# An output layer whose first groups are staged differently and an attention layer that keeps v in the matmul array

## What is computed

```python
# first block, layer 1: convolution mixer
c = layer_norm(depthwise_conv(glu(h @ w_in)))           # norm over the 1024 channels
y = (silu(c) * silu(z)) @ w_out + b_out                 # the "output layer" of this text
h = layer_norm(ALPHA * h + y)
# first block, layer 2: gated linear attention, then h = layer_norm(...)
# second block: banded attention (8 heads of 64, 2 kv heads) beside a pooling branch
def banded_attention(q, k, v, rel_bias, sink):          # blocks of 128 queries, 384 keys each
    s = where(|rel| <= 128, q @ k.T * scale + bias, -1e30)
    m = maximum(max(s), sink)
    p = exp(s - m); p = p / (sum(p) + exp(sink - m))
    return p @ v
a = banded_attention(...) * silu(gate)
x = x + rmsnorm(concat(a, pool) @ w_out)
```

## Time and profile before

| | |
|---|---|
| median of 3 runs | 2679.57 us (2676.35 to 2681.12) |
| the profiled execution, its own time | 2668.11 us |
| its span, first to last instruction | 2666.4 us |
| mean granted clock of PE | 0.964 of full |
| PE, DVE, ACT, POOL busy | 2470.5, 1361.8, 1123.5, 737.0 us |
| `conv_out`, about | 559 to 856 us of the span |
| `attn_mix`, steps of attention | 1889.9 to 2267.7 us of the span |

### The profile page before, as it was taken

One profiled execution on the slowest core, in us unless ns is written; L12 is line 12 of the kernel. 1 busy time (PEld: TensorE's weight loads), 2 busy tenths in 40 slices (PEclk: granted clock), 3 DMA queues, 4 the chain that ended last, 5 costly groups with the idle time before them and its releaser, 6 DMA issues. The chain is left out here.

```text
span 2666.4 us, 34476 instructions
## 1 busy us (share of the span) xinstructions
PE 2470.5 (93%) x13014; PEld 1330.6 (50%) x13014; DVE 1361.8 (51%) x2287; ACT 1123.5 (42%) x2180; POOL 737.0 (28%) x516
## 2 busy tenths in 40 slices
PE   7999999768998999999999998997999998898898
PEld 3555555433444455555555554443666665343343
DVE  3998888964444233434334334774355555234322
ACT  5665554455553333434334334333345544222311
POOL 0788777545776110110111010441000000000000
PEclk9999999978999999999999999998999998899899
DMA  5011110041323100100000003232200000100322
GB/s 185 25 41 54 40 40 28 16 149 59 103 95 142 52 1 5 48 1 32 13 5 9 1 1 127 95 127 59 55 17 9 8 0 1 36 16 1 128 101 94
DMA packets 48813, 134.49 MB, mean 50 GB/s; under 512 B 5071, under 2 KB 19023, under 8 KB 47640
## 3 DMA queue, kind: packets, MB, share of 16 engines
q1 hardware_dynamic: 48664, 132.47, 14.7%
HBM read 96.65 MB, written 35.80 MB: 50 GB/s over the span
## 5 line engine op out<-in xcount | busy, mean ns | idle before, releaser
L388 DVE SCALAR_TENSOR_TENSOR cm_tap_sum<-cm_glu,cm_prm,cm_tap_sum 128x2048 f32<-128x2048 f32 x168 | 395.6, 2354 | 49.2 <-ACT cm_tap_sum L246 44.5
L315 POOL TENSOR_TENSOR mixed<-mixed,cm_tap_products 128x2048 f32<-128x2048 f32 x71 | 325.7, 4588 | 88.7 <-ACT cm_tap_products L267 72.6
L90 PE MATMUL cm_proj<-H_hi,cm_w_ga_hi 128*128 128x416 f16 (+1 forms) x640 | 217.8, 340 | 21.9 <-DVE H_lo L362 18.6
L91 PE MATMUL cm_proj<-H_lo,cm_w_ga_hi 128*128 128x416 f16 (+1 forms) x640 | 217.9, 340 | 0.0
L92 PE MATMUL cm_proj<-H_hi,cm_w_ga_lo 128*128 128x416 f16 (+1 forms) x640 | 217.6, 340 | 0.0
L90 PE MATMUL gm_vr<-gm_wvr_hi,H_hi 128*128 128x512 f16 (+1 forms) x544 | 208.9, 384 | 0.0
L91 PE MATMUL gm_vr<-gm_wvr_lo,H_hi 128*128 128x512 f16 (+1 forms) x544 | 208.8, 384 | 0.0
L92 PE MATMUL gm_vr<-gm_wvr_hi,H_lo 128*128 128x512 f16 (+1 forms) x544 | 208.8, 384 | 0.0
L1389 POOL TENSOR_TENSOR gm_q_inter<-gm_q_rel,gm_block_decays 128x512 f32<-128x512 f32 x16 | 16.7, 1047 | 497.1 <-ACT gm_block_decays L1466 497.1
L1732 DVE SCALAR_TENSOR_TENSOR gm_v_r<-gm_vr,gm_v_r 128x256 f32<-128x256 f32 (+1 forms) x68 | 28.8, 424 | 243.1 <-ACT gm_v_r L1483 243.1
L260 ACT ACTIVATE cm_tap_products<-cm_glu,cm_prm 128x2048 f32<-128x2048 f32 x64 | 125.8, 1993 | 36.5 <-POOL mixed L315 36.5
(11 more groups left out here) (358 smaller groups left out, 5821.0 us busy)
## 6 DMA issues: line engine op xcount, KB each, us to landing
cm_w_stage<-conv_w SPq DMA_DIRECT2D x24, 512.0 KB, 4.0
co_rows<-x_rows SPq DMA_DIRECT2D x16, 512.0 KB, 4.4
h_rows<-co_rows SPq DMA_DIRECT2D x16, 512.0 KB, 2.9
mixed<-gla_w SPq DMA_DIRECT2D x8, 1024.0 KB, 7.0
go_rows<-h_rows SPq DMA_DIRECT2D x16, 512.0 KB, 4.0
h_rows<-go_rows SPq DMA_DIRECT2D x16, 512.0 KB, 2.8
fo_rows<-h_rows SPq DMA_DIRECT2D x16, 512.0 KB, 3.6
out<-fo_rows SPq DMA_DIRECT2D x16, 512.0 KB, 2.6
```

The source lines that it names most:

```text
L90: nc.tensor.matmul(out, w_hi, x_hi, start=first, stop=False)
L91: nc.tensor.matmul(out, w_hi, x_lo, start=False, stop=False)
L315: nc.gpsimd.tensor_tensor(c_tile(j), c_tile(j), prod[:, r % 2, :], ALU.add).then_inc(s_add, 1)
L388: nc.vector.scalar_tensor_tensor(out=acc[:, :], in0=window(j, k), scalar=col(j, k), in1=acc[:, :], op0=ALU.mult, op1=ALU.add).then_inc(s_t ...
```

## The change

In `conv_out`: the weights arrive in two transfers, columns 0 to 511 under a semaphore of their own. DVE makes both the high and the low half of the weights, the first four channel tiles before the first group's variance and the rest behind its norm. `stats` makes all eight sums of c first and then the eight sums of squares; group 1 has PSUM banks of its own for them (those of output row 1), so its sums need not wait for the norm of group 0, and output row 1 waits instead until group 1 is normed (`c_n`). The first two squares of groups 2, 3 and 4 stand ahead of the row's own work in ACT's list.

In `attn_mix`: v is the stationary operand (64 columns per head, the two heads side by side in the array) and the transposed probabilities stream past (128 columns), so the output comes out transposed and `oT` and `p_o` are gone. The division by the sum is made on the probabilities, by POOL, before they are transposed. The sink is one more column of the scores (a zero column in PSUM, the sink in the bias), so its exponential and its sum come with the others. Scores are negated, so one minimum gives the bias of the exponential. The low half is stored by POOL. The steps overlap deeper: in step U PE makes scores(U), outputs(U-3), half a projection, probsT(U-2), half a projection. All quarters project q of the next group in their first two steps and the gate in their last two; in the last group the gate is spread over four steps. All 64 steps are written out in place of the register loop.

```diff
+                sp.dma_start(w_out_room(H_hi)[:, :, 0:512], w_out_rows(next_w)[:, :, 0:512]).then_inc(ahead.half, 16)
+                ahead.load(sp, w_out_room(H_hi)[:, :, 512:D], w_out_rows(next_w)[:, :, 512:D])
...
-                def split_w(h):
-                    for k in range(KT):
-                        c = slice(h * 512, h * 512 + 512)
-                        nc.scalar.activation(w_hi[:, k, c], w_in[:, k, c], ACT.Copy, scale=WS).then_inc(s_wh, 1)
-
                 def next_squares(k):
-                    for i in ((2 * k - 8, 2 * k - 7) if k >= 4 else ()):
-                        square(1, i)
+                    if k + 2 < KT:
+                        square(1, k + 2)
                 for k in range(KT):
                     square(0, k)
-                act.wait_ge(ahead.sem, loaded)
-                split_w(0)
+                square(1, 0)
+                square(1, 1)
                 mean_square(0)
...
+                    if s in STATS:
+                        square(STATS[s], 0)
+                        square(STATS[s], 1)
...
-                    if T:
+                    if T >= 2:
                         pe.wait_ge(c_n, T * KT)
-                    else:
+                    elif T == 0:
                         pe.wait_ge(s_ones, 1)
                     for k in range(KT):
-                        nc.tensor.matmul(p_mu[:, 0:w], ones[:, :], c_tile(T, k), start=(k == 0), stop=(k == KT - 1))
+                        nc.tensor.matmul(mean(T), ones[:, :], c_tile(T, k), start=(k == 0), stop=(k == KT - 1))
+                    for k in range(KT):
                         pe.wait_ge(c_sq, T * KT + k + 1)
-                        nc.tensor.matmul(p_e2[:, 0:w], ones[:, :], sq[:, k % 2, 0:w], start=(k == 0),
+                        nc.tensor.matmul(spread_of(T), ones[:, :], sq[:, k % 2, 0:w], start=(k == 0),
                                          stop=(k == KT - 1)).then_inc(c_e2, 1)
...
+                        if s == 1:
+                            pe.wait_ge(c_n, 2 * KT)
...
+                def split_w(h, ks):
+
+                    c = slice(h * 512, h * 512 + 512)
+                    dve.wait_ge(*((ahead.half, 16), (ahead.sem, loaded))[h])
+                    for k in ks:
+                        nc.vector.tensor_scalar(w_hi[:, k, c], w_in[:, k, c], WS, None, ALU.mult).then_inc(s_wh, 1)
...
-                split_w(0)
+                split_w(0, range(KT // 2))
                 finish(0)
                 normed(0, range(KT))
-                split_w(1)
+                split_w(0, range(KT // 2, KT))
+                split_w(1, range(KT))
                 finish(1)
...
+                def divided(U):
+                    wd = band(U % NBLK)[1] * P
+                    s = sb[:, U % 3, :, 0:wd]
+                    pool.wait_ge(s_ri, U + 1)
+                    nc.gpsimd.tensor_tensor(s, s, spread(ri[:, U % 3, :], wd), ALU.mult).then_inc(s_pn, 1)
+
+                def store_lo(g):
+                    hi, lo = mixed(g)
+                    pool.wait_ge(s_hi, g + 1)
+                    nc.gpsimd.tensor_tensor(lo, og[:, :], hi, ALU.subtract).then_inc(s_lo, 1)
+                for U in range(NU + 4):
+                    if 1 <= U <= NU:
+                        divided(U - 1)
+                    if U % 4 == 3 and U >= 7:
+                        store_lo(U // 4 - 1)
...
+                        nc.scalar.activation(sb[:, r, h, 0:wd], sb[:, r, h, 0:wd], ACT.Exp, scale=-1.0,
+                                             bias=nm[:, r, h:h + 1], accum_out=sm[:, r, h:h + 1]).then_inc(s_ex, 1)
...
+                for U in range(NU + 4):
+                    p, n, g, u = step(U)
+                    if 2 <= U < NU + 2:
+                        evac_probs(U - 2)
+                    if U < NU:
+                        exps(U)
+                        last = p == QT - 1
+                        if n == 10 and not last:
+                            act.wait_ge(s_q, g + 2)
                             split(p + 2, 0, w[0])
-                        if n == 14 and not last:
-                            act.wait_ge(s_g, g + 1)
-                            split(p + 2, 1, w[0])
-                        if n < 12 and u == 1 or n == 15 and not last:
-                            q_evac(g + 1, (n // 4 + 1) % 2)
-                        if u == (3 if n < 12 else 1):
-                            gate(g, n // 4 % 2)
-                loop(act, tile)
-                evac_probs(QT * NBLK - 1, NBLK - 1)
-                store_hi(QT - 1, 3)
+                        if n == 0 and p:
+                            act.wait_ge(s_g, g)
+                            split(p + 1, 1, w[0])
+                        if u == 1 and g + 1 < NU // 4:
+                            q_evac(g + 1)
+                        if u == 3:
+                            gate(g)
+                    if u == 3 and U >= 7:
+                        store_hi(g - 1)
...
+                    for j in range(nk):
+                        for h in range(2):
+                            r = slice(h * HD, (h + 1) * HD)
+                            mm = nc.tensor.matmul(p_ot[g % 2][r, u * P:(u + 1) * P], v[:, first + j, r],
+                                                  pts[:, U % 2, h, j * P:(j + 1) * P], start=(j == 0), stop=(j == nk - 1))
...
+                for U in range(NU + 3):
+                    parts = [(), ()]
+                    if U < NU:
+                        p, n, g, u = step(U)
+                        scores(U)
+                        T, ks = n // 4, range(4 * (u % 2), 4 * (u % 2) + 4)
+                        if g + 1 == NU // 4:
+                            job, ks = (p, g, T, 1), range(2 * u, 2 * u + 2)
                         else:
-                            job = (p, g, T, 1) if u < 2 else None if last else (p + 1, g + 1, 0, 0)
-                        parts = [lambda k=k: project(*job, k) if job else None for k in (ks[:CUT], ks[CUT:])]
-                        parts[0]()
-                        if past(U - 1) is not None:
-                            oT(U - 2, g - (1 if u < 2 else 0), (n - 2) % NBLK)
-                        if past(U) is not None:
-                            probsT(U - 1, (n - 1) % NBLK)
-                        parts[1]()
-                        if past(U) is not None:
-                            outputs(U - 1, (n - 1) % NBLK)
-                loop(pe, tile)
-                U = QT * NBLK - 1
-                oT(U - 1, U // 4, NBLK - 2)
-                probsT(U, NBLK - 1)
-                outputs(U, NBLK - 1)
-                oT(U, U // 4, NBLK - 1)
+                            job = ((g + 1) // 4, g + 1, (g + 1) % 4, 0) if u < 2 else (p, g, T, 1)
+                        parts = [ks[:len(ks) // 2], ks[len(ks) // 2:]]
+                    if U >= 3:
+                        outputs(U - 3)
+                    if parts[0]:
+                        project(*job, parts[0])
+                    if 2 <= U < NU + 2:
+                        probsT(U - 2)
+                    if parts[1]:
+                        project(*job, parts[1])
...
+                    nc.vector.scalar_tensor_tensor(out=sb[:, U % 3, :, 0:wd], in0=p_s[:, :, c0:c0 + wd], scalar=-1.0,
+                                                   in1=bias[:, 2 * p:2 * p + 2, c0:c0 + wd], op0=ALU.mult,
+                                                   op1=ALU.subtract).then_inc(s_ad, 1)
...
+                    nc.vector.tensor_reduce(nm[:, r, :], sb[:, r, :, 0:wd], mybir.AxisListType.X, ALU.min).then_inc(s_nm, 1)
...
+                for U in range(NU + 4):
+                    p, n, g, u = step(U)
+                    if U < NU:
+                        biased(U)
+                    if 1 <= U <= NU:
+                        reciprocals(U - 1)
+                    if U < NU:
+                        maxima(U)
+                        if n == 10 and p < QT - 1:
+                            split(p + 2, 0, *w)
+                        if n == 0 and p:
+                            split(p + 1, 1, *w)
+                        if u == 3:
+                            gate(g)
+                    if u == 3 and U >= 7:
+                        gated(g - 1)
```

More of the change, by code:

```diff
@@ L1812, in attn_mix @@
         m = Mem(nc, ctx, "at")
+        NU = QT * NBLK
         wst = m.sb("w_stage", [P, 2, WCOLS // 2])
@@ L1899, in _ @@
                 skew = bass.AP(copies.tensor, copies.offset + P - 1, [[PITCH - 1, P], [(P + 1) * PITCH, HEADS], [1, BAND]])
[L1900 to L1905 removed]
+                sp.dma_start(bias[:, :, 0:BAND], skew).then_inc(s_bias, 16)
+                for p in range(QT - 1):
+                    load(p + 1)
             @block.gpsimd
```

289 lines of the change are left out of this document (108 added, 181 removed).

## The result

The changed kernel takes 2596.97 us (median of 4 runs, 2594.56 to 2604.89), the kernel before 2680.35 in the runs beside it (2676.35 to 2684.0): a ratio of 0.9694, 95% interval 0.9668 to 0.9721. It is 83 us faster. The forecast was 2609.0 with 2590 to 2646. The profiled execution took 2604.89 us, the slowest of its four; against the profiled 2668.11 of before the gain is only 63.2 us, where the sum had 71.

The account below looks back on a forecast made before the run. PE, busy 93% of the span, was taken to bound the kernel. Attention -54, conv_out -7 and -10 sum to -71 us; from the median 2679.57 that gives 2608.6, forecast as 2609, range 2590 to 2646.

Parts of the forecast that it names:

- Outputs: Attention steps: 12 output matmuls take 0.85 us instead of 1.38 if column halves overlap, saving 0.53 us a step.
- Rival (B): Attention outputs: column halves don't overlap, outputs cost 1.4 us; 34 us less gain, 2643 us; chance 0.17.
- The step: Attention: a regular step takes 4.95 us instead of 5.59, 0.64 less.
- the other reading: Attention steps: a third change of tiling mode drains the engine, about 0.1 us a step, 6 us less gain.
- The stalls: Attention, last quarter of each tile: one order of projections removes 19.1 us of PE stalls.
- what is late next: Attention: late bias addition in a group's fourth step costs 3 us, weight splits on DVE 2; 5 us in all.
- POOL's division: Attention: POOL divides 768 columns in 1.5 to 1.9 us, the result being needed some 5 us later.
- Rival (C): Attention: softmax chain holds each step at 5.59 us; only stalls and conv_out pay, 31 us, 2649; chance 0.09.
- conv_out, group 2: conv_out: finish(1) stays about 600, sums run during gating, row 1 starts at 625.2 against 632.73; -7 us.
- Stats(3) and (4): conv_out: sums made first cover standstills of 6.30 and 3.72 us; four fifths of the gain kept, -10 us.
- Rival (E): conv_out gains nothing, DVE's contended splits pushing norm 1 back as far as sums come forward; 2626 us; chance 0.04.
- From the profile to the median: Whole kernel: the median was assumed 11.5 us above the profiled execution, as before, turning 2597 into 2608.6.

Follow-up runs that it names:

- heads_apart: The changed kernel with one head's outputs issued wholly ahead of the other's, instead of in turn: 2609.92 us, ratio 0.9758 to the kernel before.
- old_order: The changed kernel with the earlier job order of projections put back in each tile's last quarter: 2607.36 us, ratio 0.9745 to the kernel before.
- act_splits: The changed kernel with the high halves of conv_out's weights made by ACT again, DVE making only low halves: 2596.96 us, ratio 0.9713 to the kernel before.
- conv_only: The kernel before with only the new conv_out, attention left as it was: 2648.65 us, ratio 0.9909 to the kernel before.
- pe_pad: The changed kernel with 64 two-column matmuls added on PE ahead of k's projections: 2597.1 us, ratio 0.9718 to the kernel before.

## Why the prediction held, and where its sizes were off

**The bound.** PE's list set the time before and after, at 93%. The gain came from a shorter list (38 us of the 63 in the profiles) and from standstills in it (25), as argued from the earlier trace rows.

**Outputs.** The term 0.85 us measured 0.81. The reason given, that the column halves overlap as the row halves of the scores pair do, is half right: heads_apart shows 0.27 us for it, and the other 0.30 comes without any overlap, with weights of 64 columns in place of 128. So the size was right for a reason that is only half so. Rival (B) was priced at 1.4 us a step and 34 us; without the interleaving the cost is 1.08 and 12 to 15 us. The upper part of the range rested on a price that was twice too high.

**The step.** 4.95 predicted, 5.00 measured. The missing 0.09 stands between the last projection and scores, where outputs had stood before. The Trainium skill (TensorEngine Tiling (Array Packing), Key Properties) says that a change of tiling mode drains the engine. The trace agrees in so far as scores, the first matmuls on half the rows, start 0.31 us behind a float16 matmul, and full-array float32 transposes 0.21; no run varies the mode alone. The 0.1 that I had set beside the sum as the other reading was the better one for this place; outputs and scores gave back half of it.

**The stalls and what is late next.** 19.1 us were to go, 16 in the first three tiles and 3 in the last. old_order brings back 11.0 in the first three, so the one order of projections is what removed at least these; the shorter chain around them may have the other 5. In the last tile they did not all go: 1.92 us stand in step 60. The term for what is late next was 5 us; measured are 0.51 us in three places, 1.5, and 0.11 us in eight steps. My count of the fourth step of a group was late by 0.2 us where the trace has room. 0 to 63: 304.9 predicted, 307.24 measured: some 3 us for the 0.05 a step and the 1.92 of step 60, against 2.6 us too many for what is late. The end of attention grew by 1.6 us, not 3.5. Together -53.6 against -54, closer than its terms: that is luck.

**POOL's division.** 1.47 us, at the foot of 1.5 to 1.9, and hidden. On DVE it costs 5 us. Rival (C), a softmax chain that holds each step at 5.59, has nothing for it: between 1905 and 1994 PE is busy for 88.50 of 89 us, DVE for 41, ACT for 50 and POOL for 30.

**conv_out, group 2.** Row 1 was put at 625.2 and came at 623.77; finish(1) at 600 and came at 598.92. The sum of the splits was right at 19.3 us against 19.6, by errors that cancel: the twelve high halves, counted as free of POOL (0.45), take 0.77 to 0.87 beside it, 4.5 us more; the low halves take 1.16 beside POOL where 1.7 was counted, and 0.61 alone, 2.8 us less; and the 2 us set apart for the row's bias on POOL are in these figures already, since it ran beside the high halves. That ACT's shorter chain is spent there held in act_splits.

**Stats(3) and (4).** This is the mis-sized term: "POOL ... catches up only during stats, so I keep four fifths", 10 us. Measured are 22.0 - 9.0 = 13.0, all of the 12.3 that the rows gave. The discount for POOL had no row behind it. In all conv_out gave 22 where 17 were predicted. Rival (E), nothing from conv_out, falls with conv_only.

**The setup.** "The setup ends on the same bias transfer" missed 9.5 us in the profiled execution, the standstills in v's projections. No standstill in the trace of before pointed to them.

**From the profile to the median.** The sum made 2597 for the profiled execution and added 11.5 for the median, as before had it. It came the other way: the profiled execution was 7.9 above the median. Six of the seven other runs of the changed kernel lie between 2590.8 and 2599.2, one at 2603.7; the two profiled ones at 2604.9 and 2605.6. That looks as if most unprofiled runs had no standstill in v. The other kernels agree: where the profile has the standstill, the profiled execution is 3.7 to 10.1 us above the median of its kernel (nine profiles, two of them of the changed kernel); where it has none, 0.1 to 11.5 below (five). But unprofiled runs leave no trace, and it isn't shown. The 11.5 of before rested on three runs. In the runs beside the experiments, on three other chips, the kernel before has medians of 2672.2 to 2672.9, only 4 to 5 above its profile, and single runs of 2663.4 to 2689.0. So the sum's 2608.6 missed 2596.97 by 11.6 us: 5 from conv_out's term and 19.4 from the step to the median (+11.5 assumed, -7.9 found), less 9.5 for the standstill in v and 3.3 of small terms (the steps 2.4 short, their end 1.9 better, 2.9 given back in unchanged stages). The mechanisms were right; the step from the profiled execution to the median was the worst-founded term of the sum, and that the forecast came within 12 us owes something to errors that cancel.

## What to carry to other kernels

Where a wait is periodic, look in the order in which two engines' lists meet, before looking for a faster operation: one order of projections and sums made ahead of squares gave some 11 us each, more than the transposes that fell away (0.11 us a step, 7 in all). A discount on a gain needs a row as much as the gain does. And when the profiled execution and the median disagree, compare stretches of unchanged code first: a change can move a standstill into a stage that it doesn't touch.

## What the runs showed of the hardware that was not expected

- Short matmuls (128 columns, float16, 18 a microsecond with their loads) stand still for 2.8 to 7.4 us, waiting for no engine, while a 2064 KB transfer of some 50 GB/s runs; 64 matmuls more ahead of them remove it in one kernel and bring it on in the other, and without the transfer it is gone. They wait for a 16 KB packet of their own instructions, one for 128 matmuls, and go on 1.3 to 1.6 us after it lands (17 of 17 standstills).
- A standstill costs more than itself: in old_order 2.33 us of waiting are followed by matmuls at 0.43 us apart in place of 0.22, the granted clock of that step is 0.81, at its lower level (1.2 GHz) for part of it, and the step takes 9.07 us where its twins with the same wait take 7.38. The wait of 1.92 us in step 60 leaves a step of 5.68 us in the changed kernel, at a granted clock of 1.00, and one of 7.22 in pe_pad, where the clock of the 10 us around it is 0.83.
- Beside POOL a DVE split with one input slows from 0.36 to between 0.77 and 0.87 us, one with two from 0.62 to 1.16, and POOL's own gating from 0.70 to 0.89 and 1.15. The Trainium skill (SBUF — State Buffer, SBUF: two separate sides) calls the shared port an exclusive lock for DVE operations in a two-port mode or with two inputs; of the operations with one input no run here shows whether they were in such a mode.
- A float32 matmul with 64 columns of weights and 128 streaming takes 0.090 us a record alone and 0.068 in turn with the other half of the array.
